# Prompt attention of a hybrid decoder on one core: scores and mixing as three float32r products, query staging moved to ScalarE and GpSimd, odd pages loaded later

## What is computed

```python
def mla_core(q_lat, q_rope, c, kr, q_pos, k_pos):
    s = jnp.einsum('bhtr,bsr->bhts', q_lat, c) + jnp.einsum('bhtp,bsp->bhts', q_rope, kr)
    s = s.astype(jnp.float32) * SOFTMAX_SCALE
    s = jnp.where(k_pos[None, :] <= q_pos[:, None], s, jnp.finfo(jnp.float32).min)
    p = jax.nn.softmax(s, axis=-1).astype(c.dtype)
    return jnp.einsum('bhts,bsr->bthr', p, c)
```

## Time and profile before

| | us |
|---|---|
| median of 3 runs | 2235.38 |
| the profiled execution | 2231.13 |
| its span | 2229.5 |
| TensorE busy, share of the span | 2012.7, 90% |
| VectorE busy, share | 904.8, 41% |
| ScalarE busy, share | 641.8, 29% |
| GpSimd busy, share | 126.1, 6% |

### The profile page before, as it was taken

One profiled execution on the slowest core, in us unless ns is written; L12 is line 12 of the kernel. 1 busy time (PEld: TensorE's weight loads), 2 busy tenths in 40 slices (PEclk: granted clock), 3 DMA queues, 4 the chain that ended last, 5 costly groups with the idle time before them and its releaser, 6 DMA issues. The chain is left out here.

```text
span 2229.5 us, 51187 instructions
## 1 busy us (share of the span) xinstructions
PE 2012.7 (90%) x22040; PEld 1797.7 (81%) x22040; DVE 904.8 (41%) x1491; ACT 641.8 (29%) x1057; POOL 126.1 (6%) x167
## 2 busy tenths in 40 slices
PE   4789889998899999995799889999998899999995
PEld 3656557776899999994699759988944899999995
DVE  5323541223253433335943164445253353333334
ACT  2112434443142212222533333333120232212222
POOL 0001000340000000000000020000131000000000
PEclk7889999998999999997899989999885999999998
DMA  4012401783223232321222100001030222232321
GB/s 125 20 51 71 138 0 44 244 245 117 59 77 92 76 95 85 89 72 27 59 82 76 29 2 4 4 4 41 4 102 19 67 76 85 77 100 79 89 72 40
DMA packets 229240, 158.06 MB, mean 71 GB/s; under 512 B 12504, under 2 KB 221247, under 8 KB 228928
## 3 DMA queue, kind: packets, MB, share of 16 engines
q1 hardware_dynamic: 223412, 136.93, 20.8%
q0 software_dynamic: 5376, 18.36, 2.7%
q10 hardware_dynamic: 268, 0.08, 0.0%
HBM read 149.96 MB, written 5.34 MB: 70 GB/s over the span
## 5 line engine op out<-in xcount | busy, mean ns | idle before, releaser
L311 PE MATMUL ps<-ffn_xh,ffn_wh 128*128 128x280 f32 x1408 | 299.0, 294 | 18.0 <-DVE ffn_xl L1360 13.7
L311 PE MATMUL ps<-ffn_xh,ffn_wl 128*128 128x280 f32 x1408 | 297.2, 292 | 0.0
L311 PE MATMUL ps<-ffn_xl,ffn_wh 128*128 128x280 f32 x1408 | 296.3, 292 | 0.0
L311 PEld LDWEIGHTS ps<-ffn_xh,ffn_wh 128*128 128x128 f32 x1408 | 225.8, 190 | 19.0 <-issue 18.8
L311 PEld LDWEIGHTS ps<-ffn_xh,ffn_wl 128*128 128x128 f32 x1408 | 225.6, 190 | 0.0
L311 PEld LDWEIGHTS ps<-ffn_xl,ffn_wh 128*128 128x128 f32 x1408 | 224.6, 190 | 0.0
L1262 ACT CAST ffn_wh<-wa 128x1024 fp32r<-128x1024 f32 x88 | 91.3, 1041 | 208.0 <-PE ps L311 180.4
L311 PE MATMUL ps<-ffn_hid_h,ffn_wh 128*128 128x280 f32 x704 | 148.0, 291 | 0.0
L311 PE MATMUL ps<-ffn_hid_h,ffn_wl 128*128 128x280 f32 x704 | 147.6, 291 | 0.0
L311 PE MATMUL ps<-ffn_hid_l,ffn_wh 128*128 128x280 f32 x704 | 147.5, 291 | 0.0
L317 DVE TENSOR_TENSOR ffn_wl<-wa,ffn_wh 128x1024 fp32r<-128x1024 f32 x88 | 107.7, 1225 | 87.2 <-ACT ffn_wh L1262 87.2
(11 more groups left out here) (355 smaller groups left out, 3625.5 us busy)
## 6 DMA issues: line engine op xcount, KB each, us to landing
wa<-in_ffn_w_gate SPq DMA_DIRECT2D x44, 512.0 KB, 3.7
wa<-in_ffn_w_up SPq DMA_DIRECT2D x44, 512.0 KB, 3.7
arena<-in_cache SPq DMA_DIRECT2D x77, 160.0 KB, 3.4
wb<-in_ffn_w_down SPq DMA_DIRECT2D x16, 768.0 KB, 4.6
wb<-in_ffn_w_down SPq DMA_DIRECT2D x16, 640.0 KB, 4.3
arena<-in_cache POOLq DMA_DIRECT2D x63, 160.0 KB, 3.5
wb<-in_cache SPq DMA_DIRECT2D x40, 160.0 KB, 3.5
wb<-in_cache POOLq DMA_DIRECT2D x28, 160.0 KB, 3.6
```

The source lines that it names most:

```text
L311: mm = nc.tensor.matmul(dst[:, s, 0:HALF], a[:, c * width:(c + 1) * width], b[:, c, s * HALF:(s + 1) * HALF], start=first and n == 0, stop ...
```

## The change

Scores and mixing of the prompt are each computed as three float32r products instead of one float32 product.

- Keys and latent rows are split once, at the start of the block: `kh`, `vh` by ScalarE, `kl`, `vl` by VectorE. They lie in `wb` and `wa`, where the odd sample's pages lay.
- The query of a tile is split as it is staged: `stage_high` on ScalarE, `stage_low` on GpSimd. `stage` on VectorE is gone. ScalarE's place for it is behind `exponents(i + 1)` and ahead of `keep_mixed(i)`.
- The turned probabilities are split: ScalarE's `keep_turned` writes `pTh`, and a new `lower_turned` on VectorE writes `pTl`; TensorE's mixing waits for the latter. It stands behind `mask_and_max(i + 1)` and ahead of `weigh(i + 1)`.
- In the attention all 32 pages of sample 0 are loaded by SyncE and none by GpSimd. The pages of sample 1 are loaded at the start of the decode, half on each queue, ahead of those of sample 2.

```diff
--- before.py
+++ after.py
@@ -643,7 +644,7 @@
         page_pool = [[sem(f"page_pool{u}_{g}") for g in range(PAGES // GP)] for u in range(2)]
-        first_sp, first_pool, then_sp, then_pool = (0, 1, 2), (3,), (0, 2), (1, 3)
+        first, then_sp, then_pool = (0, 1, 2, 3), (0, 2), (1, 3)
         page_used = [[sem(f"page_used{u}_{g}") for g in range(PAGES // GP)] for u in range(2)]
@@ -674,8 +675,15 @@
         probs, hat = part(hat, 2, TP)
-        probsT, hat = part(hat, 2, 5 * P)
-        qst, hat = part(hat, 2, 3, P)
+
+        qsh, qsl = as_r("p_qsh", "hT", hat, 2, 3, P), as_r("p_qsl", "hT", hat + 6 * P, 2, 3, P)
+        hat += 12 * P
+        kh, kl = as_r("p_kh", "wb", 0, 3, T), as_r("p_kl", "wb", 3 * T, 3, T)
+        vh, vl = as_r("p_vh", "wb", 6 * T, 5, KL), as_r("p_vl", "wa", 0, 5, KL)
+        pTh, pTl = as_r("p_pTh", "wa", 5 * KL, 2, 5 * P), as_r("p_pTl", "wa", 5 * KL + 10 * P, 2, 5 * P)
+        assert 6 * T + 5 * KL <= wb.all.shape[1] and 5 * KL + 20 * P <= wa.all.shape[1]
+        k_high, k_low, v_high, v_low, staged_high, turned_high = (
+            sem(f"p_{n}") for n in ("k_high", "k_low", "v_high", "v_low", "staged_high", "turned_high"))
@@ -704,7 +712,10 @@
                     k = P if c < 2 else ROPE
-                    mm = nc.tensor.matmul(ps[:, b, 0:n], qst[0:k, u, c], kT[0:k, c, a:a + n], start=c == 0, stop=c == 2)
+                    if isinstance(i, int) and i == 0:
+                        pe.wait_ge(k_low, c + 1)
+                    for m, (x, y) in enumerate(((qsh, kh), (qsh, kl), (qsl, kh))):
+                        mm = nc.tensor.matmul(ps[:, b, 0:n], x[0:k, u, c], y[0:k, c, a:a + n], start=c == 0 and m == 0, stop=c == 2 and m == 2)
             mm.then_inc(scored, 1)
         def turn_and_mix(pe, i, u, g):
@@ -719,10 +730,14 @@
             ge(pe, mixed_kept, i - 1)
+            if isinstance(i, int) and i == 0:
+                pe.wait_ge(v_low, 2)
             for c in range(RC):
                 for j, n in chunks_of(g):
-                    mm = nc.tensor.matmul(ps[:, 5 + u, c * P:(c + 1) * P], ctok[0:n, j, c * P:(c + 1) * P],
-                                          probsT[0:n, u, j * P:(j + 1) * P], start=j == 0, stop=j == chunks_of(g)[-1][0])
+                    for m, (x, y) in enumerate(((vh, pTh), (vh, pTl), (vl, pTh))):
+                        mm = nc.tensor.matmul(ps[:, 5 + u, c * P:(c + 1) * P], x[0:n, j, c * P:(c + 1) * P],
+                                              y[0:n, u, j * P:(j + 1) * P], start=j == 0 and m == 0,
+                                              stop=j == chunks_of(g)[-1][0] and m == 2)
             mm.then_inc(mixed, 1)
         def keep_below(act, i, u, g):
@@ -738,8 +753,15 @@
             if g == 4:
-                nc.scalar.copy(probsT[0:TAIL, u, n:n + P], ps[0:TAIL, 7, 0:P])
-            nc.scalar.copy(probsT[:, u, 0:n], ps[:, 3 + u, 0:n]).then_inc(turned_kept, 1)
+                nc.scalar.copy(pTh[0:TAIL, u, n:n + P], ps[0:TAIL, 7, 0:P])
+            nc.scalar.copy(pTh[:, u, 0:n], ps[:, 3 + u, 0:n]).then_inc(turned_high, 1)
+
+        def lower_turned(dve, i, u, g):
+            ge(dve, turned_high, i + 1)
+            n = min(g + 1, 4) * P
+            if g == 4:
+                take_low(pTl[0:TAIL, u, n:n + P], ps[0:TAIL, 7, 0:P], pTh[0:TAIL, u, n:n + P])
+            take_low(pTl[:, u, 0:n], ps[:, 3 + u, 0:n], pTh[:, u, 0:n]).then_inc(turned_kept, 1)
         def exponents(act, i, u, g):
@@ -753,14 +775,25 @@
-        def stage(dve, i, u):
-
-            ge(dve, scored, i - 1)
+        def stage_rows(i):
             for c in range(3):
                 k = P if c < 2 else ROPE
-                cp = nc.vector.tensor_copy(qst[0:k, u, c].rearrange("p (t h) -> p h t", h=H),
-                                           q[0:k, c, :, bass.ds(i * QT, QT)])
-            cp.then_inc(staged, 1)
+                yield c, k, q[0:k, c, :, bass.ds(i * QT, QT)]
+
+        def stage_high(act, i, u):
+
+            ge(act, scored, i - 1)
+            for c, k, src in stage_rows(i):
+                cp = nc.scalar.copy(qsh[0:k, u, c].rearrange("p (t h) -> p h t", h=H), src)
+            cp.then_inc(staged_high, 1)
+
+        def stage_low(pool, i, u):
+
+            ge(pool, staged_high, i + 1)
+            for c, k, src in stage_rows(i):
+                low = nc.gpsimd.tensor_tensor(qsl[0:k, u, c].rearrange("p (t h) -> p h t", h=H), src,
+                                              qsh[0:k, u, c].bitcast(F32).rearrange("p (t h) -> p h t", h=H), ALU.subtract)
+            low.then_inc(staged, 1)
         def mask_and_max(dve, i, u, g, a):
@@ -810,15 +843,19 @@
                 sp.wait_ge(ptab_in, 16)
-                load_pages(sp, 0, first_sp, page_sp)
-                load_pages(sp, 1, first_sp, page_sp)
+                load_pages(sp, 0, first, page_sp)
                 sp.wait_ge(cnew_in, 16 * DB)
             @block.gpsimd
             def _(pool):
-                pool.wait_ge(ptab_in, 16)
-                load_pages(pool, 0, first_pool, page_pool)
-                load_pages(pool, 1, first_pool, page_pool)
+                stage_low(pool, 0, 0)
+                stage_low(pool, 1, 1)
+
+                def step(i, u, g, gn, an):
+                    if not isinstance(i, int) or i + 2 < NT:
+                        stage_low(pool, i + 2, u)
+                over_tiles(pool, step)
+                pool.wait_ge(staged, NT)
             @block.tensor
             def _(pe):
@@ -832,6 +869,14 @@
             @block.scalar
             def _(act):
+                for c in range(3):
+                    k = P if c < 2 else ROPE
+                    nc.scalar.copy(kh[0:k, c, 0:TP], kT[0:k, c, 0:TP]).then_inc(k_high, 1)
+                    if c == 0:
+                        stage_high(act, 0, 0)
+                nc.scalar.copy(vh[:, 0:4], ctok[:, 0:4, 0:KL])
+                nc.scalar.copy(vh[0:TAIL, 4], ctok[0:TAIL, 4, 0:KL]).then_inc(v_high, 1)
+                stage_high(act, 1, 1)
                 exponents(act, 0, 0, 0)
                 def step(i, u, g, gn, an):
@@ -840,6 +885,8 @@
                         exponents(act, i + 1, 1 - u, gn)
+                    if not isinstance(i, int) or i + 2 < NT:
+                        stage_high(act, i + 2, u)
                     keep_mixed(act, i, u, g)
@@ -866,16 +913,21 @@
-                stage(dve, 0, 0)
-                stage(dve, 1, 1)
+                for c in range(3):
+                    k = P if c < 2 else ROPE
+                    dve.wait_ge(k_high, c + 1)
+                    take_low(kl[0:k, c, 0:TP], kT[0:k, c, 0:TP], kh[0:k, c, 0:TP]).then_inc(k_low, 1)
+                dve.wait_ge(v_high, 1)
+                take_low(vl[:, 0:4], ctok[:, 0:4, 0:KL], vh[:, 0:4]).then_inc(v_low, 1)
+                take_low(vl[0:TAIL, 4], ctok[0:TAIL, 4, 0:KL], vh[0:TAIL, 4]).then_inc(v_low, 1)
                 mask_and_max(dve, 0, 0, 0, 0)
...
                 def step(i, u, g, gn, an):
-                    if not isinstance(i, int) or i + 2 < NT:
-                        stage(dve, i + 2, u)
                     if gn is not None:
                         mask_and_max(dve, i + 1, 1 - u, gn, an)
+                    lower_turned(dve, i, u, g)
+                    if gn is not None:
                         weigh(dve, i + 1, 1 - u, gn)
@@ -922,14 +974,14 @@
             @block.sync
             def _(sp):
-                for b in range(2, DB):
+                for b in range(1, DB):
                     load_pages(sp, b, then_sp, page_sp)
...
             @block.gpsimd
             def _(pool):
-                for b in range(2, DB):
+                for b in range(1, DB):
                     load_pages(pool, b, then_pool, page_pool)
             @block.tensor
@@ -937,8 +989,10 @@
                 def turn_latents(b, g, half):
...
                     if g * 4 % GP == 0 and half == 0:
-                        pe.wait_ge(page_sp[b % 2][g * 4 // GP], GP // 4 * 16 * (len(first_sp) + b // 2 * len(then_sp)))
-                        pe.wait_ge(page_pool[b % 2][g * 4 // GP], GP // 4 * 16 * (len(first_pool) + b // 2 * len(then_pool)))
+
+                        turn = (b + 1) // 2
+                        pe.wait_ge(page_sp[b % 2][g * 4 // GP], GP // 4 * 16 * (turn * len(then_sp) + (len(first) if b % 2 == 0 else 0)))
+                        ge(pe, page_pool[b % 2][g * 4 // GP], GP // 4 * 16 * turn * len(then_pool))
                     ge(pe, lat_copied, 2 * (n - 1) + half + 1)
```

More of the change, by code:

```diff
@@ L196, in program @@
         rs = sb("rs", [P, 2, HALF])
+        here("wa")
         wa = Ring(ctx, nc, "wa", 4, DC * P)
@@ L902, in program @@
         omix, hat = part(hat, RC, P)
-        assert hat <= 4 * TP + 2 * 5 * P + 6 * P
+        assert hat <= 4 * TP + 12 * P
         kts, _ = carve(q_end, 2, 8, P)
```

## The result

| us | before | after |
|---|---|---|
| median of 4 runs | 2234.23 | 2388.74 |
| lowest and highest | 2231.09, 2235.84 | 2385.14, 2393.52 |
| the profiled execution | 2231.13 | 2393.52 |
| its span | 2229.5 | 2391.9 |
| mean granted clock of TensorE | 0.942 | 0.886 |

The changed kernel takes 154.5 us more, a ratio of 1.0705 (95% interval 1.0687 to 1.0723). The forecast was +70, its range ended at 2356. The loss lies in the prompt's attention, which takes 298 us for 147; its start is 4 us later, so the decode begins 155.7 us later than before, and it is as long as it was to within 0.7 us. The profiled execution is the longest of the four, 5 us above their median; some 6 us of its 162 us lie behind the decode, where the granted clock in 1156 to 1556 us was 0.91 for 0.92 and in 1556 to 1956 us 0.89 for 0.90.

A forecast was written before the change was run, and what follows sets the result against it. TensorE was taken to run the prompt's attention without slack; new query and probability links add 63 us over its steps, head 3.5 and tail 3, pages nothing: 70 us, giving 2305 us, range 2278 to 2356.

The forecast's parts named there:

- Both links: Prompt's attention: GpSimd's query low half releases early scores, VectorE's probabilities low half late mixing; steps +2.7 to +1.65 us.
- The mixing's start at +2.80: Step with 512 keys: mixing starts 2.80 us after the scores' end, not 1.40, behind VectorE's mask and subtraction.
- Narrow record 0.111: Scores and mixing: a float32r record of 128 columns takes 0.111 us, between 0.064 and 0.222.
- Steps of 5.0, 5.7, 6.4 and 7.9 us: Attention loop: forecast step lengths with 128, 256, 384 and 512 keys, adding 63 us over 31 steps.
- Two terms of staging: Query staging: ScalarE's three casts 0.75 us, GpSimd's three subtractions of 128 columns 1.0 us.
- The hand-off terms: Query staging: 0.1 us at each hand-off, within 2.05 us from the exponential's end to the next scores.
- Pages at nothing: Start of the decode: loading sample 1's 32 pages there costs nothing, as the DMA engines are idle.
- Head and tail: Attention's start, splitting keys and values: +3.5 us; its last tile, more mixing records and later mixings: +3 us.
- an added risk: Clock in the seven steps with 128 keys: if all run at 1.2 GHz, scores about 1 us longer each, +7.
- Rival 1: Scores and mixing: narrow float32r costs like float32, 0.222 us per 128 columns; 51 us more, 2356; chance 0.16.
- Rival 3: Scores and mixing: faster, each product saving one of four passes, 22 us in all, 2213 us; chance 0.06.

The follow-up runs named there:

- the first experiment: Changed kernel with unread float32 products put into TensorE's waits for the staged query and for the low half of the turned probabilities: 2317.52 us, ratio to before 1.039.
- the last two experiments: Kernel before with late pages and float32r only in wide scores, low halves kept: from 384 keys on 2227.72 us (0.9983), from 256 on 2228.82 us (0.9987).
- the links with float32: Changed kernel with all its splitting and waits, but each product one float32 product again, low halves left out: 2344.91 us, ratio to before 1.0512.
- no links: Changed kernel with three float32r products but the query staged at its old place, mixing waiting for ScalarE's copy alone, two low halves left out: 2292.28 us (1.0269).

## Why the prediction was wrong

The sign was right, the size by far not. Step by step:

- **The order of the waits held.** Both links came as named: GpSimd releases the scores with 128 keys, VectorE's subtraction the mixing with 512. The mixing's start at +2.80 was 2.60 in the changed kernel and 2.71 with the clock up.
- **Prices at 2.4 GHz held.** Narrow record 0.111: 0.11. Record of 512 columns 0.224: 0.23. Scores at 512 keys 2.39: 2.46. Steps of 5.0, 5.7, 6.4 and 7.9 us: 5.35, 6.1 to 6.25, 7.0 and 7.85 in the first experiment. There the decode begins 92 us later than before, for the forecast's 70. Of the 22 us between them some 9 lie in the steps with 128 to 384 keys at 2.4 GHz, 4 in a longer head and some 7 in the few steps at the low clock (0.62 in 206 to 224 us, 0.50 in 262 to 271 us). How much of it is the fillers' own time no run separates.
- **Two terms of staging were too small.** GpSimd's three subtractions took 1.47 us for 1.0, 0.49 each, more than halfway from the 0.33 that I took to the upper end of 0.6; ScalarE's three casts 0.88 for 0.75. The hand-off terms covered a part: exponential to scores was 2.39 for 2.05.
- **Pages at nothing held**: 1.0008, and sample 1 was turned 16.1 us into the decode for 14.7, in a decode that is 0.7 us longer.
- **Head and tail**: the first score record came 4.1 us later, for +3.5. From the last tile's transposes to the decode it took 11.0 us for 5.6, +5.4 for +3; in the first experiment 8.3, which is the forecast's +3.
- **The step that failed is the clock.** It stood in the prediction as "an added risk", priced at +7: seven steps with 128 keys, and their scores alone. It was in force from the first tile, without a break to 393 us and for most of the rest, on scores, transposes and mixing alike. Counted from the span's start, the decode begins at 509.1 us in the changed kernel, at 445.4 with the clock brought back (the first experiment) and at 353.4 before. So some 64 of 156 us went with the clock; single steps show it too: 12.15 us for 7.85 with 512 keys, 9.55 for 7.0 with 384. By these starts the forecast lacked 86 us: these 64, and the 22 that stay in the first experiment with its fillers.
- **Why I missed it.** I tied the clock to TensorE's idle time with 128 keys, read from the earlier trace rows, and did not ask what the 1.2 to 1.4 us longer wait before each later mixing would do, nor whether the clock would come back up. And I had only a price of time for a narrow float32r record, none for its effect on the clock, which no row of before could show.
- **Rival 1 looked right and was not.** Its 0.222 us per narrow record is in the trace (0.213), and a sum with it gives 2356, nearer the result than mine. But a record of 512 columns doubled too, and with work in the waits both went back. Its nearness to the result is luck. A price seen at one clock is no price of the product.
- **Rival 3's gain exists**, in the last two experiments, where the hand-offs are hidden, but it is 0.1 to 0.2% of the time, not 1%.

What is shown: longer pauses cost the clock with float32 products too (the links with float32, the filler taken away); float32r products in scores and mixing cost it without new pauses (no links), scores alone only at the start, mixing alone mostly at the end; unread work in the pauses brings most of it back. What is open: why a stream of short float32r records without a gap is left at 1.2 GHz. The runs do not separate the number of columns per record, the number of records and the product's kind. Nor do they separate filling a pause from what fills it, as every filler was a float32 product of 384 or 512 columns; one of short float32r records was not tried.

## What to carry to other kernels

Price the clock for every record of a stage, not for the one stretch in which a pause is new: here waits 1.2 us longer ahead of the mixing, a new wait in the early steps and shorter products kept TensorE at 1.2 GHz for most of 300 us, and that made some 64 of the 156 us lost. Read the granted clock of the stage before calling a record slow; an unread product in the wait is a cheap test, and sometimes a fix. Splitting a float32 product into three float32r ones paid here (0.2%) where the moving operand was wide and the low half was made well ahead of its use, and not where 128 columns are multiplied or the low half stands between transposes and mixing of the same tile.

## What the hardware showed that I had not expected

- TensorE with 30.00 us busy in 30.00 was granted 0.50 throughout (float32r without the links, 220 to 250 us).
- Records follow the granted clock, by nearly the factor of two: narrow float32r ones lie 0.213 us apart at 0.50 and 0.111 at 1.00, those of 512 columns 0.43 and 0.23.
- Removing one unread product per step made the kernel before 8 us slower.
- A GpSimd subtraction of 128 columns takes about 0.5 us (three in 1.47, the last alone 0.51), half of what 512 columns take.
